# Hybrid decoder step on one core: conditioning rows turned on VectorE, page units ahead of the position products, another order at the sample attention's entry

## The chip, the cores and the metric

One core of a Trainium2 chip runs one layer of a hybrid decoder step in one launch. The metric is the device time of the whole launch in microseconds (us); lower is better.

## The reference, cut to what matters

The layer runs for a prompt of 512 tokens and for 8 samples of 8 tokens each (64 tokens), which share the weights. The conditioning vectors `c` (one of the prompt, eight of the samples) give shifts, scales and gates; the samples attend to past keys in pages.

```python
def adaln(c, w_ada, b_ada):
    mod = jax.nn.silu(c) @ w_ada + b_ada
    return jnp.split(mod[:, None, :], 6, axis=-1)

def compress(rows, pe, w1, w2):                    # over 2048 + 8 cached rows of each sample, and over the prompt
    chunks = rows[:, :n_ch * CMP_STRIDE].reshape(...)
    proj = jnp.einsum('bnkf,rfh->rbnkh', chunks, w1.reshape(r_n, CMP_STRIDE * HEAD_DIM, CMP_HIDDEN))
    pre = sum(proj[r][:, r:r + nc] for r in range(r_n)) + pe.reshape(-1) @ w1
    out = jax.nn.silu(pre) @ w2
...
    q, kc_r, vc_r, ks, vs, kw, vw, gates, u, bg = project(modulate(xs, ln1_g, sh1, sc1), pos_s, w_in, q_norm_g, k_norm_g)
    # attention: compressed blocks, 16 selected blocks of 64 keys, a window of 512; mixed by gates
    o = nsa_attend(q, pos_s, kc, vc, kc_end, ksb, vsb, kw_all, vw_all, kw_pos, gates)
    cy, s_conv = short_conv(u, state_conv, w_conv)
    xs = xs + g1 * mix_out(o, bg * cy, attn_out_g, conv_out_g, w_o)     # each part RMS-normed first
    xs = xs + g2 * swiglu(modulate(xs, ln2_g, sh2, sc2), w_gu, w_down)
```

## The kernel before

Each engine has one program, written in order by hand; engines wait for one another by semaphores. A PSUM bank is one of eight; `plan_banks` fixes for every product (a key such as `("pre", 3)`) which bank it takes and as whose successor. `want_free`, `want_filled` and `want_emptied` are waits on a bank's predecessor, its product and its evacuation; `fills` and `frees` give the marks. So an order in `plan_banks` is also an order of waits.

**Start, 0 to 130 us.** Sixteen page units u (keys and values of 8 samples in turn, 1 MB each) go through: GpSimd gathers a unit by four indirect DMAs into one of four slots (line 892), and from unit 4 on waits until unit u-4 has been turned; VectorE turns it in squares of 32 (`turn_chunks`, line 1602) into one of two buffers; TensorE forms its products with the first compression weights (`compress_first`, line 2506); ScalarE copies one half (line 1059), VectorE adds the other (`both_chunks`, line 1608), ScalarE takes the silu with the bias `pebt` (line 1067); TensorE forms the second products (`compress_second`, line 2514). Among the units stand: `turn_rows`, which turns silu(c) (`scrow`, 9 rows of 1024) by eight turns on TensorE into `cT`, and the gain rows into `colT`; `position_rows` (line 2494), 32 products of one column with 64 weight columns each that give the bias `pebt`, between units 0 and 1; eight steps with `w_ada` (line 2467), the turns of the normed tokens (line 2432), and in VectorE's step 13 the modulation of all tokens. Then come the projections with pairs of high and low weights (lines 2438 to 2440), first of attention, then of the convolution (`cv`, n 0 to 2, m 0 to 3, two halves h).

**Middle, 250 to 292 us.** During the last third (n = 2: the gate blocks `("cv", 2, m, h)`) the work of the sample attention begins between the blocks: units 16 and 17 (the prompt's), queries placed, compressed scores, their softmax (`cmp_probs`), its turn (`cmp_turn`) and values. VectorE multiplies each block into `vT` (line 1861) and gives `y_ready`; ScalarE squares it. `turn_page(gp, b)` (line 1826) turns a page of selected keys; (0, 0) overwrites the compression weights and so waits for unit 17's products. Behind the last block TensorE makes the query copies `qR`, importance and values, turns the new keys (`kTn`), and sums the squares of the convolution output (`yss`, line 2830); ScalarE takes the roots. Then `scores(0)` (line 2708).

**Groups, 288 to 380 us.** Four groups gp of two samples: scores, window scores, exponentials on ScalarE (line 1238), turned probabilities `("PT", gp, i)`, compressed scores of the next group, importance (`imp`, line 1800), ranking, two steps with `w_ada`, next scores, values. Group 0 also holds the norm of the prompt's compressed keys (`norm_inverse(2)`, `norm_apply(11)`, lines 1697 to 1719) and their turn (`turn_blocks(2)`). SP's queue loads tokens, weights and states; it waits in order too.

## Time and profile before

| | us |
|---|---|
| three runs | 923.3, 924.52, 925.25 (median 924.52) |
| the profiled execution's own time | 924.75 |
| its span, first to last instruction | 922.9 |
| TensorE busy | 854.2 (93%) |
| VectorE, ScalarE, GpSimd busy | 622.8, 372.8, 307.5 |

In the page's slices each digit is a fortieth of the span, 23 us. In a timeline row the bracket names how long the engine stood idle just before and what ended that; "remote" or "issue" means that the profile shows no releaser. Recorded ends of products on TensorE are modelled.

### The profile page before, as it was taken

How to read it: one execution, taken by the hardware profiler on the slowest of the kernel's cores; microseconds unless marked ns; L12 is line 12 of the kernel's file. 1: busy time of each engine (PE TensorE's matmuls, PEld its weight loads, DVE VectorE, ACT ScalarE, POOL GpSimd, SP SyncE). 2: the span in 40 equal slices, each digit the busy share in tenths (PEclk: the TensorE clock that was granted, in tenths of full speed). 3: DMA queues.
4: the chain of work that ended last, by engine and by line, in shares of the span. 5: the costliest groups of instructions: out<-in, count | busy, mean ns of one | idle time of the engine just before them, and what ended most of it. 6: DMA issues, size and time to landing. Idle time of an engine off the chain costs nothing.

```text
span 922.9 us, 17110 instructions
## 1 busy us (share of the span) xinstructions
PE 854.2 (93%) x6689; PEld 733.0 (79%) x6689; DVE 622.8 (67%) x1219; ACT 372.8 (40%) x751; POOL 307.5 (33%) x303
## 2 busy tenths in 40 slices
PE   3498999999988789899999998999999999999998
PEld 2366778899976556676777798999999999888886
DVE  2156585388945775758486899888888888434444
ACT  1033252141234343767843664444444446223221
POOL 6465400000003321535500318777766773000000
PEclk9699999999988788999999999999999999999999
DMA  7988913236276798294102453333333324422201
GB/s 207 344 306 313 317 47 99 94 110 243 68 263 249 277 376 301 51 316 138 36 1 92 129 147 107 98 101 104 95 93 93 93 92 153 156 92 92 74 1 52
DMA packets 89166, 138.88 MB, mean 150 GB/s; under 512 B 9267, under 2 KB 59987, under 8 KB 84798
## 3 DMA queue, kind: packets, MB, share of 16 engines
q1 hardware_dynamic: 74866, 96.26, 32.6%
q0 software_dynamic: 9376, 40.31, 12.2%
q10 hardware_dynamic: 4844, 1.21, 0.6%
q8 instruction: 54, 0.88, 0.4%
q14 instruction: 26, 0.21, 0.1%
HBM read 130.58 MB, written 11.31 MB: 154 GB/s over the span
## 4 chain that ended last, share of the span: by engine, by line
PE 78%; DVE 8%; issue 7%; ACT 3%; another core or an unknown queue 1%; POOL 1%; DVEq 0%; ACTq 0%; POOLq 0%
PE bank L2438 18%; PE bank L2440 18%; PE bank L2439 18%; PE bank L2432 4%; PE bank L2506 4%; PE bank L2794 2%; PE bank L2708 2%; PE bank L2926 2%; PE bank L2467 2%; PE bank L2448 2%; PE bank L2447 2%; PE bank L2958 2%; PE bank L2764 1%; DVE mem L1602 1%
## 5 line engine op out<-in xcount | busy, mean ns | idle before, releaser
L2438 PE MATMUL bank<-s,ring_hi 128*128 128x288 f32 x620 | 184.7, 298 | 3.7 <-DVE ring_lo L536 3.7
L2439 PE MATMUL bank<-s,ring_lo 128*128 128x288 f32 x620 | 183.6, 296 | 0.0
L2440 PE MATMUL bank<-s,ring_hi 128*128 128x288 f32 x620 | 183.0, 295 | 0.0
L2438 PEld LDWEIGHTS bank<-s,ring_hi 128*128 128x128 f32 x620 | 116.8, 188 | 4.6 <-DVE ring_lo L536 4.5
L2440 PEld LDWEIGHTS bank<-s,ring_hi 128*128 128x128 f32 x620 | 117.5, 190 | 0.0
L2439 PEld LDWEIGHTS bank<-s,ring_lo 128*128 128x128 f32 x620 | 117.0, 189 | 0.0
L536 DVE TENSOR_TENSOR ring_lo<-mem,ring_hi 128x512 fp32r<-128x512 f32 x84 | 106.3, 1301 | 2.1 <-POOL mem L988 1.8
L536 DVE TENSOR_TENSOR dn_w<-wring,dn_w 128x2048 fp32r<-128x2048 f32 (+1 forms) x11 | 23.1, 2096 | 65.9 <-ACT dn_w L533 65.9
L2438 PE MATMUL bank<-dn_w,dn_hi 128*128 128x512 f32 x160 | 62.2, 389 | 0.0
L2439 PE MATMUL bank<-dn_w,dn_lo 128*128 128x512 f32 x160 | 62.2, 389 | 0.0
L2440 PE MATMUL bank<-dn_w,dn_hi 128*128 128x512 f32 x160 | 62.2, 389 | 0.0
L901 POOL DMA_INDIRECT arena<-in_cache_k_slc,idx x8 | 7.9, 988 | 157.3 <-PE bank L2440 148.1
L2438 PE MATMUL bank<-hhi,ws 128*128 128x288 f32 x192 | 58.0, 302 | 0.0
L2439 PE MATMUL bank<-h1hi,ws 128*128 128x288 f32 x192 | 57.6, 300 | 0.0
L2440 PE MATMUL bank<-h1hi,ws 128*128 128x288 f32 x192 | 57.6, 300 | 0.0
L533 ACT CAST dn_w<-wring 128x2048 fp32r<-128x2048 f32 (+1 forms) x11 | 19.3, 1757 | 83.0 <-PE bank L2440 83.0
L536 DVE TENSOR_TENSOR ring_lo<-wring,ring_hi 128x512 fp32r<-128x512 f32 x71 | 52.4, 743 | 0.5 <-ACT ring_hi L533 0.5
L533 ACT CAST ring_hi<-mem 128x512 fp32r<-128x512 f32 x84 | 49.9, 617 | 6.5 <-POOL mem L980 2.3
L980 POOL TENSOR_TENSOR mem<-wring 128x512 f32<-128x512 f32 x20 | 26.8, 1338 | 55.6 <-PE bank L2440 31.9
L533 ACT CAST ws<-wring 128x1024 fp32r<-128x1024 f32 (+2 forms) x18 | 21.8, 1246 | 48.4 <-PE bank L2448 27.2
L892 POOL DMA_INDIRECT arena<-in_cache_k_cmp,idq x32 | 31.5, 984 | 27.9 <-DVE uvT L1602 15.4
L533 ACT CAST ring_hi<-wring 128x512 fp32r<-128x512 f32 x71 | 39.8, 616 | 0.0
(444 smaller groups left out, 2126.5 us busy)
## 6 DMA issues: line engine op xcount, KB each, us to landing
wring<-in_w_gu SPq DMA_DIRECT2D x44, 512.0 KB
wring<-in_w_ada SPq DMA_DIRECT2D x16, 1024.0 KB
wring<-in_w_in SPq DMA_DIRECT2D x10, 1024.0 KB
wring<-in_w_down SPq DMA_DIRECT2D x10, 1024.0 KB
wring<-in_w_ada SPq DMA_DIRECT2D x16, 512.0 KB
proj<-in_x_prompt SPq DMA_DIRECT2D x4, 512.0 KB
mem<-in_state_k_win POOLq DMA_DIRECT2D x8, 256.0 KB
mem<-in_state_v_win POOLq DMA_DIRECT2D x8, 256.0 KB, 7.5
```

The lines of the kernel that those rows point to most:

```text
L533: return copy(dst, src)
L536: return eng.tensor_tensor(dst, src, hi.bitcast(F32), ALU.subtract)
L892: pool.indirect_dma_start(cring[:, slot_of(i), 512 * n:512 * n + 512], None, a[name].rearrange("l n (c i s) k d -> (l n c i) (s k d)", i=4 ...
L980: ins = pool.tensor_tensor(dst, block_of(f, 0), block_of(f, 1), ALU.subtract)
L2432: return pe.transpose(dst, src, ident[0:P, 0:P])
L2438: pe.matmul(dst, sh, ml, start=first and k == 0, stop=False)
L2439: pe.matmul(dst, sl, mh, start=False, stop=False)
L2440: ins = pe.matmul(dst, sh, mh, start=False, stop=last and k == len(pairs) - 1)
L2447: pe.matmul(dst, s, ml, start=first and k == 0, stop=False)
L2448: ins = pe.matmul(dst, s, mh, start=False, stop=last and k == len(pairs) - 1)
L2467: ins = pe.matmul(ps(key)[32 * j:32 * j + 32, :], cT[:, 32 * kk:32 * kk + 32], w[:, j, :], start=kk == 0, stop=kk == 7)
L2506: ins = pe.matmul(dst, w1v[:, u % 2, j].rearrange("p r h -> p (r h)"), x[:, j // 2, j % 2], start=j == 0, stop=j == 7)
```

## The change

Conditioning rows: `crow` is laid out as 128 x 256 (four groups of 32 partitions, nine used in each), loaded by eight DMAs of SP in place of two, cleared first by VectorE; one VectorE transpose of it makes `cT`. ScalarE issues the value weights ahead of the gain rows. Start: VectorE turns two units ahead and does so first in each step; units 0 to 2 stand ahead of the position products, which are 16 of 128 weight columns by 2 columns, and whose two parts VectorE adds; second products run two units behind. Middle: the turn of the first key page is moved from m = 1 to the end of m = 2, that of the second in between the last block's two halves; the turn of the new keys stands before the importance; query copies stand before the last square on ScalarE. The squares are summed fully by VectorE ahead of TensorE, and TensorE's sum, the roots and the norm's root move into group 0, behind the turned probabilities; `norm_apply(11)` and `turn_blocks(2)` move to group 1. Two exponentials of one column are added on ScalarE.

```diff
@@ -146,18 +146,19 @@
-        if u == 0:
-            start += [("cT",), ("rows",)]
...
-        if u == 0:
+        if u == 1:
+            start.append(("rows",))
+        if u == 2:
...
-        if u:
-            start.append(("cmp", u - 1))
+        if u >= 2:
+            start.append(("cmp", u - 2))
+    start.append(("cmp", 14))
@@ -173,8 +174,7 @@
-                    ring += [("qR", i) for i in range(4)] + [("imp", 0)]
-    ring += [("kTn",), ("yss", 0), ("yss", 1)]
+                    ring += [("qR", i) for i in range(4)] + [("kTn",), ("imp", 0)]
@@ -189,8 +189,8 @@
-            ring += [("PT", gp, i) for i in range(4)] + [("cPT", gp + 1)] + [("PT", gp, i) for i in range(4, 6)] + [("imp", gp + 1)]
-            ring += [("kct", 2)] * (gp == 0) + keyed(gp + 1)
+            ring += [("PT", gp, i) for i in range(4)] + [("cPT", gp + 1)] + [("PT", gp, i) for i in range(4, 6)]
+            ring += [("yss", h) for h in range(2)] * (gp == 0) + [("imp", gp + 1)] + [("kct", 2)] * (gp == 1) + keyed(gp + 1)
@@ -312,7 +312,7 @@
-        crow, scrow = hbuf[0:9, 2 * D:3 * D], hbuf[0:9, D:2 * D]
+        crow, scrow = hbuf[:, 2048:2304], hbuf[:, 1024:1280]
@@ -372,7 +372,7 @@
-        pebt = sb("pebt", 2, parts=64)
+        pebt = sb("pebt", 4, parts=64)
@@ -682,8 +682,11 @@
-            sp.dma_start(crow[0:1, :], a["c_prompt"]).then_inc(c_loaded, 16)
-            sp.dma_start(crow[1:9, :], a["c_sample"]).then_inc(c_loaded, 16)
+            sp.wait_ge(c_cleared, 1)
+            for q in range(4):
+                for r0, n, name in ((0, 1, "c_prompt"), (1, 8, "c_sample")):
+                    sp.dma_start(crow[32 * q + r0:32 * q + r0 + n, :].rearrange("b (k r) -> b k r", r=32),
+                                 a[name].rearrange("b (k q r) -> q b k r", q=4, r=32)[q]).then_inc(c_loaded, 16)
@@ -1029,6 +1032,9 @@
+            hidden_load(1)
+            for x, w in enumerate(("w_ck2", "w_cv2")):
+                act.dma_start(w2[:, 64 * x:64 * x + 64], a[w][0]).then_inc(comp_w_loaded, 16)
@@ -1042,11 +1048,8 @@
-            hidden_load(1)
-            for x, w in enumerate(("w_ck2", "w_cv2")):
-                act.dma_start(w2[:, 64 * x:64 * x + 64], a[w][0]).then_inc(comp_w_loaded, 16)
...
-            act.wait_ge(c_loaded, 32)
+            act.wait_ge(c_loaded, 128)
@@ -1064,6 +1067,8 @@
+                if u < 2:
+                    want_emptied(act, ("peb", u))
@@ -1183,6 +1188,10 @@
+                if m == 3:
+                    for i in range(4):
+                        want_filled(act, ("qR", i))
+                        frees(act.copy(qR[i // 2][i % 2], ps(("qR", i))[:, 0:256]), ("qR", i))
@@ -1216,15 +1225,8 @@
-            for i in range(4):
-                want_filled(act, ("qR", i))
-                frees(act.copy(qR[i // 2][i % 2], ps(("qR", i))[:, 0:256]), ("qR", i))
...
-            nrm(2)
-            for h in range(2):
-                want_filled(act, ("yss", h))
-                frees(act.activation(yrs[:, HALF * h:HALF * h + HALF], ps(("yss", h))[:, 0:HALF], ACT.Sqrt,
-                                     bias=epst[:, 0:1], scale=1.0 / 512), ("yss", h))
+            act.activation(small[:, 253:254], small[:, 252:253], ACT.Exp, scale=-1.0)
@@ -1251,6 +1253,13 @@
+                    nrm(2)
+                    for h in range(2):
+                        want_filled(act, ("yss", h))
+                        frees(act.activation(yrs[:, HALF * h:HALF * h + HALF], ps(("yss", h))[:, 0:HALF], ACT.Sqrt,
+                                             bias=epst[:, 0:1], scale=1.0 / 512), ("yss", h))
+                    act.activation(small[:, 253:254], small[:, 252:253], ACT.Exp, scale=-1.0)
+                if gp == 1:
@@ -1513,11 +1522,11 @@
+            dve.memset(crow, 0.0).then_inc(c_cleared, 1)
...
-            link(dve.memset(cT[:, :], 0.0))
@@ -1610,17 +1619,21 @@
+            turn_chunks(1)
...
-                if u < 15:
-                    turn_chunks(u + 1)
-                if u >= 2:
-                    cmp_evac(u - 2)
-                if u == 0:
-                    evac(("cT",), cT[:, :].rearrange("p (k r) -> p k r", r=32)[:, :, 0:9],
-                         ps(("cT",))[:, 0:72].rearrange("p (k r) -> p k r", r=9))
+                if u < 14:
+                    turn_chunks(u + 2)
+                if u >= 3:
+                    cmp_evac(u - 3)
+                if u == 1:
...
+                    dve.wait_ge(scrow_ready, 1)
+                    dve.transpose(cT[:, :], scrow).then_inc(c_turned, 1)
...
-                        evac(("peb", x), pebt[:, x:x + 1], ps(("peb", x))[64 * x:64 * x + 64, 0:1])
+                        want_filled(dve, ("peb", x))
+                        link(dve.tensor_copy(pebt[:, 2 + x:3 + x], ps(("peb", x))[64:128, 1:2]))
+                        frees(dve.tensor_tensor(pebt[:, x:x + 1], pebt[:, 2 + x:3 + x], ps(("peb", x))[0:64, 0:1], ALU.add),
+                              ("peb", x))
@@ -1646,6 +1659,7 @@
+            cmp_evac(13)
@@ -1856,6 +1870,8 @@
+                    if m == 3 and h:
+                        turn_page(0, 1)
@@ -1870,7 +1886,6 @@
-                    turn_page(0, 0)
@@ -1881,10 +1896,12 @@
+                    turn_page(0, 0)
...
+            evac(("kTn",), kTn, ps(("kTn",))[:, 0:128].rearrange("p (x n) -> p x n", x=2))
@@ -1972,11 +1989,12 @@
-            turn_page(0, 1)
-            evac(("kTn",), kTn, ps(("kTn",))[:, 0:128].rearrange("p (x n) -> p x n", x=2))
...
+            dve.wait_ge(y_square, 4)
+            dve.tensor_tensor(yrs, hcT[:, 2, :], hcT[:, 3, :], ALU.add).then_inc(y_summed, 1)
+            dve.wait_ge(y_summed, 3)
@@ -2009,7 +2027,7 @@
-                if gp == 0:
+                if gp == 1:
@@ -2472,29 +2490,19 @@
-                pe.wait_ge(scrow_ready, 1)
-                want_free(pe, ("cT",))
-                for k in range(8):
-                    ins = turn(ps(("cT",))[:, 9 * k:9 * k + 9], scrow[:, 128 * k:128 * k + 128])
-                fills(ins, ("cT",))
...
-                pe.wait_ge(comp_w_loaded, 160)
-                want_emptied(pe, ("cT",))
...
-                ins = [None, None]
-                for i in range(16):
-                    for x in range(2):
-                        ins[x] = pe.matmul(ps(("peb", x))[64 * x:64 * x + 64, 0:1], w1v[:, x, i % 8, i // 8, :], colT[:, 36 + i:37 + i],
-                                           start=i == 0, stop=i == 15)
-                for x in range(2):
-                    fills(ins[x], ("peb", x))
+                    for j in range(8):
+                        ins = pe.matmul(ps(("peb", x))[:, 0:2], w1v[:, x, j].rearrange("p r h -> p (r h)"),
+                                        colT[:, 36:52].rearrange("p (r j) -> p j r", r=2)[:, j], start=j == 0, stop=j == 7)
+                    fills(ins, ("peb", x))
@@ -2541,11 +2549,16 @@
+                    pe.wait_ge(comp_k_loaded, 128)
+                if u == 1:
+                    pe.wait_ge(comp_w_loaded, 160)
+                compress_first(u)
+                if u == 1:
...
-                    pe.wait_ge(comp_k_loaded, 128)
-                compress_first(u)
-                if u == 0:
+                if u == 2:
...
+                if u == 4:
+                    pe.wait_ge(c_turned, 1)
@@ -2554,8 +2567,9 @@
-                if u:
-                    compress_second(u - 1)
+                if u >= 2:
+                    compress_second(u - 2)
+            compress_second(14)
@@ -2681,12 +2695,11 @@
+                            want_free(pe, ("kTn",))
+                            for x, c in enumerate((TKS, TKW)):
+                                ins = turn(ps(("kTn",))[:, 64 * x:64 * x + 64], pj[0:TS, 4, c:c + 128])
+                            fills(ins, ("kTn",))
...
-            want_free(pe, ("kTn",))
-            for x, c in enumerate((TKS, TKW)):
-                ins = turn(ps(("kTn",))[:, 64 * x:64 * x + 64], pj[0:TS, 4, c:c + 128])
-            fills(ins, ("kTn",))
@@ -2740,6 +2753,7 @@
+                want_emptied(pe, ("kTn",))
@@ -2821,18 +2835,16 @@
-            pe.wait_ge(y_summed, 2)
-            pe.wait_ge(y_square, 4)
-            for h in range(2):
-                key = ("yss", h)
-                want_free(pe, key)
-                for m in range(2, 4):
-                    last = pe.matmul(ps(key)[:, 0:HALF], cst[:, C_ONE:C_ONE + 128], hcT[:, m, HALF * h:HALF * h + HALF],
-                                     start=m == 2, stop=m == 3)
-                fills(last, key)
+            def sum_conv():
+                pe.wait_ge(y_summed, 3)
+                for h in range(2):
+                    key = ("yss", h)
+                    want_free(pe, key)
+                    fills(pe.matmul(ps(key)[:, 0:HALF], cst[:, C_ONE:C_ONE + 128], yrs[:, HALF * h:HALF * h + HALF],
+                                    start=True, stop=True), key)
...
-            want_emptied(pe, ("kTn",))
@@ -2849,10 +2861,12 @@
+                    if gp == 0:
+                        sum_conv()
...
-                    if gp == 0:
+                    if gp == 1:
```

## Rows read from the trace of the kernel before

**Rows 1.** The page: TensorE's busy time, and its busy tenths in 40 slices.
```profile
PE 854.2 (93%) x6689; PEld 733.0 (79%) x6689; DVE 622.8 (67%) x1219; ACT 372.8 (40%) x751; POOL 307.5 (33%) x303
...
PE   3498999999988789899999998999999999999998
```

**Rows 2.** Busy times by stage: window, us, then each engine, clock, DMA share, GB/s.
```profile
24.50:38.40 13.90, 1.16 (x9) 1.17 (x7) 0.00 (x0) 0.00 (x0) 7.52 (x8) 0.57 0.95 325
...
80.00:100.00 20.00, 20.00 (x117) 14.49 (x117) 13.02 (x18) 4.52 (x11) 12.40 (x12) 0.97 0.88 311
...
268.70:273.40 4.70, 0.10 (x2) 0.11 (x1) 3.65 (x9) 1.73 (x3) 0.00 (x0) 0.88 0.53 165
273.40:282.80 9.40, 9.40 (x53) 9.24 (x53) 4.58 (x12) 0.95 (x3) 0.00 (x0) 0.70 0.01 2
```

**Rows 3.** Timeline of TensorE at the start: start us, us, line, what.
```profile
17.16 6.63 PE L2506 MATMUL bank<-uvT,mem 128*128 128x256 f32 x16
23.72 0.86 PE L2494 MATMUL bank<-colT,mem 128*64 128x1 f32 x22
...
38.40 2.10 PE L2494 MATMUL bank<-colT,mem 128*64 128x1 f32 x36 [1.94 <-issue]
40.43 5.25 PE L2506 MATMUL bank<-mem 128*128 128x256 f32 x16
```

**Rows 4.** Timelines of ScalarE, SP and GpSimd at the start.
```profile
38.50 0.37 ACT L1059 COPY arena<-bank 64x254 f32<-64x254 f32 x1 [22.61 <-remote]
...
21.86 7.16 SPq L767 DMA_DIRECT2D proj<-in_x_prompt  x4
...
43.69 0.95 POOL L892 DMA_INDIRECT arena<-in_cache_k_cmp,idq  x1 [9.54 <-DVE uvT L1602]
```

**Rows 5.** Timelines of VectorE and TensorE before the last block.
```profile
268.41 2.31 DVE L1826 STREAM_TRANSPOSE mem<-arena 128x2048 f32<-128x2048 f32 x1 [7.91 <-PE bank L2506]
...
272.57 0.21 DVE L1608 TENSOR_TENSOR arena<-arena,bank 64x62 f32<-64x62 f32 x1 [0.95 <-ACT arena L1059]
...
266.48 1.89 PE L2506 MATMUL bank<-uvT,mem 128*128 128x64 f32 x16
...
273.32 0.55 PE L2432 MATMUL bank<-cst,uvT 128*127 128x128 f32 x1 [4.61 <-DVE uvT L1789]
```

**Rows 6.** ScalarE, TensorE and VectorE at the entry, and the first scores' window.
```profile
286.76 0.87 ACT L1226 ACTIVATE mem<-bank,epst 128x288 f32<-128x288 f32 x2
...
294.33 1.28 ACT L1238 ACT_TABLE_LOAD   x1
...
284.45 2.18 PE L2830 MATMUL bank<-arena,cst 128*128 128x288 f32 x8
288.09 0.58 PE L2708 MATMUL bank<-mem 32*32 32x512 f32 x1 [1.46 <-ACT mem L1226]
...
291.12 0.69 DVE L1904 CUSTOM_DVE_ANT_1 arena<-bank,selb 128x512 f32<-128x512 f32 x1 [3.22 <-PE bank L2708]
...
288.10:292.00 3.90, 3.90 (x66) 1.30 (x68) 0.88 (x3) 0.00 (x0) 1.98 (x2) 1.00 0.98 396
```

**Rows 7.** VectorE's last page transpose but one, TensorE's unit 13 and first projection product.
```profile
112.87 2.30 DVE L1602 STREAM_TRANSPOSE uvT<-arena 128x2048 f32<-128x2048 f32 x1
...
112.98 3.72 PE L2506 MATMUL bank<-mem 128*128 128x256 f32 x16
...
126.34 0.50 PE L2438 MATMUL bank<-ws,h1hi 128*128 128x512 f32 x1
```

**Rows 8.** VectorE's norm and importances in the groups, TensorE's second scores, ScalarE.
```profile
303.83 0.15 DVE L1697 RECIPROCAL hss<-hrt 128x2 f32<-128x2 f32 x1
...
326.87 0.19 DVE L1800 TENSOR_SCALAR imps<-bank 128x30 f32<-128x30 f32 x1 [0.38 <-PE bank L2633]
...
306.84 0.58 PE L2708 MATMUL bank<-mem 32*32 32x512 f32 x1 [1.20 <-DVE imps L1800]
...
305.68 0.18 ACT L1168 COPY mem<-bank 128x31 f32<-128x31 f32 x1 [3.06 <-PE bank L2432]
```

4 lines of the change are left out of this document (2 added, 2 removed).

## The prediction

> **What bounds the kernel now.** I read the page first [rows 1]: TensorE is busy 93% of the span, and the two places where its line in the slices drops are the first slice pair and the slices from 260 to 350 us. Both are where the change works, so I read those two stretches alone, by the busy times in windows [rows 2]. In 24.5 to 38.4 us TensorE is busy for 1.16 us of 13.9. In 268.7 to 273.4 us it is busy for 0.10 of 4.7, and the stretch behind that has a mean granted clock of 0.70, so that part of it ran at the lower of the two levels. From 400 us on TensorE is hardly ever idle, so a start that is earlier by some time should end the kernel earlier by as much.
>
> At the start the timeline [rows 3] shows the first page unit's products (17.16), then position products that begin at 23.72 and are all through only at 40.43. They have no wait between them; between 24.5 and 38.4 they trickle. ScalarE shows what is behind it [rows 4]: its copy of unit 0 needs only that unit's products, which are recorded as over at 23.79, yet it runs at 38.50 after 22.61 us of idle. So it is not the position products' own work that costs the time (the 36 behind 38.40 take 2.10 us, with no gap). Completions of TensorE reach the others late while GpSimd's gathers are under way: GpSimd had stood for 9.54 us when it went on at 43.69 [rows 4], so its burst of issues ended at 34.1, some 4 us before things moved again.
>
> In the middle the timeline [rows 5] shows VectorE's transpose of the first key page at 268.41: it had stood in front since 260.5, waiting for the products of unit 17, and with it stood the evacuation of the third gate block, which unit 17's hidden rows and the softmax product wait for. TensorE's turn at 273.32 waited 4.61 us for that product. At the entry [rows 6] TensorE is held until 288.09 by ScalarE's second square root, which frees the bank that the scores take (0.87 us for both roots, and a table load ahead of them). Behind it the exponentials of group 0 wait for another table load of 1.28 us at 294.33.
>
> **The change, part by part.**
>
> *Conditioning rows.* Eight turns on TensorE (about 1 us) and a copy go, a VectorE transpose of 256 columns comes. Transposes of 2048 columns take 2.30 us [rows 7], so it costs about 0.3 us, and between nothing and 0.7 in any case; it lies in VectorE's idle start. The two loads become eight, in runs of 128 bytes, on SP's queue ahead of the token loads. These wait for a gathered page and are issued from 21.86 us [rows 4], so even at 0.7 us an issue all eight are gone by 7 us. ScalarE issues the same loads in another order and is free for the silu no later. Nil.
>
> *Position products.* 32 products with 64 loaded columns become 16 with 128: the same number of loaded columns, so about the same 2 us without a stall. Half the instructions would matter if each is held for a fixed time, but they now stand behind unit 2, after the stall. Nil, bounds -1 and +1 us.
>
> *Units ahead.* Unit 0 starts when its transpose is done, some 1.5 us earlier, but is still published only when the stall ends. I keep 38.4 for that, since the gathers up to unit 5 are issued without waiting on TensorE. By then unit 1 has run too: the 5.25 us of unit 1 [rows 3] are saved. Against it: unit 2 needs VectorE's transpose, which now starts at 38.4 (2.3 us, unit 2 at 40.8, where unit 1 stood before). Then come position products (2 us), the position bias (two instructions in each of two halves on VectorE, 0.9 us), silu and the second product of unit 0 (1.5 us), and only then unit 3, at about 49.5 where it stood at 50.42. Net gain here 0.9 us. The two-unit lag of the second products spares the wait of about 1 us that one finds at later stalls: together some 2 us.
>
> *The end of that stage.* The transpose of unit u+2 now stands ahead of everything that VectorE does in step u. In step 13 this is the last transpose, and it waits for unit 13's products (over at 116.70, where the transpose before it ran at 112.87 and the modulation followed without a wait), ahead of the modulation of all tokens [rows 7]. VectorE was without a gap from 112.5 to 127 and fed the first projection at 126.34 in time; now it idles 1.6 us. I count +1.7 us. So the whole start gives about -0.3 us, which is a difference of terms that are each larger: I take 0, bounds -7.5 (two units of 3.72 us and no loss behind) and +5.
>
> *First key page moved behind the gates.* Now the evacuation of the third block runs at once. From the copy of unit 17 at 272.24 to the turn at 273.32 is 1.08 us; this chain (ScalarE's copy runs from 272.24) can start at 268.4, when the unit's products are done [rows 5]. The turn then comes at 269.5: -3.8 us. TensorE idles 1 us in place of 4.6, and I assume the clock stays at the upper level. The stretch 273.4 to 282.8 at a mean of 0.70 [rows 2] is then 9.4 x 0.70 = 6.6 us: -2.8 us. The last block is filled at about 276.3, 6.4 us earlier. What is late next is VectorE: from 269.5 it has an evacuation (0.3), the norm's sum (0.6), groups (0.6), gates (1.5), the page (2.3), sums of squares (1.55) and an evacuation (0.5), end at 277.1. That takes back 0.8 us.
>
> *The entry.* Before, scores began 5.4 us behind the last block's end. Now behind 277.1: the second page (2.3; it was behind the evacuation), evacuation and its mark (0.6), the key turn on TensorE (0.33) and its copy with the unit's (0.5), importance and value products (0.7): 4.4 us, scores at 281.5 in place of 288.09. Gone are the squares' four products (2.18 us, they are two of 1.1 later) and the wait on ScalarE. The extra sum on VectorE (0.78) lies in its wait of 3.22 us for the scores [rows 6]. Entry and block together: -6.6 us. GpSimd's value and window loads hang on the last block's end and come earlier with it; VectorE's wait for the first window was nil and stays so.
>
> *What is pushed into the groups.* In group 0 TensorE gets the two sum products (1.1 us) behind the turned probabilities, ScalarE a table load, a root, two roots of 0.87 together and a load back (3.7 us, most of it in the 3.06 us before 305.68 in which it stood idle [rows 8]), and VectorE loses the norm of 1.6 us that stood in front of the importance [rows 8]. The table for the exponentials is now loaded early, by an exponential of one column in ScalarE's idle time; the 1.28 us go from the path, but TensorE's window scores in front of the turned probabilities let it come only 0.5 us earlier. Scores of group 1 waited 1.20 us for the importance; they then wait for TensorE alone, some 305.65 for 306.84: -1.2 us. In group 1 the norm comes in behind the groups' product, in front of the window's transpose and the importance, where VectorE had 0.38 us free [rows 8]; the last score bank is now the one that importance frees: +1.3 us. Sum +0.1 us.
>
> The sum: 0 - 6.6 + 0.1 = -6.5 us. The profiled execution took 924.75 us, 0.2 above the median of 924.52; 924.75 - 6.5 = **918.2 us**.
>
> **The rivals.**
>
> *The start pays too.* If unit 0 is published before the stall sets in (its products now end at 22.3), VectorE turns unit 2 at once, and two units are done when the stall ends. Their 7.4 us come on top: 910.8. For it: the stall is seen only from 23.8 on. Against: the mark of unit 0 was among those held back, and it now stands at nearly the same time.
>
> *The clock takes it back.* The new entry leaves TensorE with little to do from 276.8 to 281.5. If it falls to the lower level there, the scores (3.9 us at the old place [rows 6], at the upper level) take some 2.3 us more; if it falls already for the 1 us idle before the last block, 2.8 us are lost again. With both the gain is 1.4 us: 923.3, no change that can be measured. For it: the level fell within a stretch of 4.7 us idle and lasted into the products. The Trainium skill's page "TensorE: Matmul & The Clock Gate", in its part on the clock gate, says that the array drops to half rate when it has been little used and comes back only after sustained use; by that rule the moved work is best where TensorE keeps busy, and the change removes filler from the entry.
>
> *Slower: the gathers don't pause.* Before, the gathers paused from 34.2 to 43.69, and the completions came through within that pause. If unit 2 is turned during the stall, GpSimd follows at once with unit 6 (four issues, 5 us), and the stall lasts 5 us longer; each later burst, now closer to its predecessor, can do that again. With two such prolongations the start loses 10 us against the 6.5 won: 928.2. It decides from 6.5 us of prolongation on. Against it: TensorE could run ahead during a stall, and in 80 to 100 us, with gathers throughout, it was busy all the time [rows 2].
>
> *The stage behind swallows it.* Pages and windows load the DMA engines at 0.98 around 290 us [rows 6]. If the values of the first groups wait for pages and these are no earlier, some 5 us go: 923.2.
>
> **How the numbers follow.** Forecast 0.52 (914.5 to 921.5, all but 0.01 faster); the start pays 0.20; the clock 0.10; swallowed 0.08; slower 0.10. A measurement tells about 0.2% (1.85 us) from no change. Faster: 0.51 + 0.20 and half of the swallowed case, 0.74; same: 0.15; slower: 0.11. The range goes from the paying start (910.8) to just above the unchanged time, 925.5; it leaves out most of the slower case and a start that pays still more.
>
> **What would show it.** First key page's transpose at about 272.8 with the turn of the softmax at 269.5, no idle stretch above 1.5 us before the last block, granted clock 1.00 there, scores 6 to 7 us earlier against the first projection's start. In group 1 the second scores wait for the importance. At the start the first projection within 2 us of 126.3, ScalarE's first copy still at about 38. If that copy comes at 23 us or at 43, the term for the start is wrong; if the first scores take 4.5 us or more, it is the clock.

## The result, and the profile after

| | before | after |
|---|---|---|
| runs of one comparison, us | 923.3 to 925.25, median 924.16 (4) | 933.18, 934.5, 938.34, 938.59, median 936.42 |
| profiled execution, own time, us | 924.75 | 933.18 |
| its span, us | 922.9 | 931.3 |

The changed kernel is slower: ratio 1.0135, 95% interval 1.0112 to 1.0158, that is 12.3 us, where the prediction said 6.5 us faster. The traced execution of after is the fastest of its four: its span is 8.4 us longer than that of before's trace, so the account below explains 8.4 us; the 3.9 us from there to the difference of the medians stand in executions that aren't traced. The page of after is nearly that of before [rows 1]: TensorE is busy 5.2 us more, and its slices say no more than that the first stage is a little emptier.

```profile
PE 859.4 (92%) x6645; PEld 735.0 (79%) x6645; DVE 624.8 (67%) x1222; ACT 373.4 (40%) x754; POOL 307.3 (33%) x303
...
PE   3298989999997788999999998999999999999998
```

So I compare the same step in both timelines. These are the rows of before that the earlier groups don't hold: TensorE's units 3 and 12, and ScalarE's first exponential in groups 0 and 1.

```profile
50.42 3.72 PE L2506 MATMUL bank<-mem 128*128 128x256 f32 x16
...
108.31 3.72 PE L2506 MATMUL bank<-uvT,mem 128*128 128x256 f32 x16
...
295.63 1.15 ACT L1238 ACTIVATE arena<-arena,small 128x1024 f32<-128x1024 f32 x1
...
312.05 1.15 ACT L1238 ACTIVATE arena<-arena,small 128x1024 f32<-128x1024 f32 x1 [5.83 <-DVE small L1989]
```

| step | before | after | difference |
|---|---|---|---|
| unit 3, products | 50.42 | 53.94 | +3.5 |
| unit 12, products | 108.31 | 115.68 | +7.4 |
| first projection [rows 7] | 126.34 | 140.08 | +13.7 |
| unit 17, products [rows 5] | 266.48 | 281.49 | +15.0 |
| exponentials of group 0 | 295.63 | 304.21 | +8.6 |
| of group 1 | 312.05 | 319.17 | +7.1 |
| of group 2 | 332.23 | 340.37 | +8.1 |
| end of the span | 922.9 | 931.3 | +8.4 |

The table splits the change in two. The start loses 13.7 us (15.0 at unit 17; the first projections ran at a lower clock). From unit 17 on the kernel wins 6.6. First the start of after: ScalarE (line 1062 is the copy of before's line 1059, 1072 the silu), VectorE (1611 is the turn of units, 1534 a copy out of a bank), GpSimd's gathers (895), TensorE (2503 position products, 2514 units).

```profile
23.93 0.37 ACT L1062 COPY arena<-bank 64x254 f32<-64x254 f32 x1 [6.91 <-remote]
50.03 0.51 ACT L1072 ACTIVATE arena<-arena,pebt 64x254 f32<-64x254 f32 x1 [25.74 <-issue]
...
23.87 2.31 DVE L1611 STREAM_TRANSPOSE uvT<-arena 128x2048 f32<-128x2048 f32 x1 [3.10 <-remote]
...
43.53 2.31 DVE L1611 STREAM_TRANSPOSE mem<-arena 128x2048 f32<-128x2048 f32 x1 [17.05 <-remote]
45.76 0.17 DVE L1534 COPY colT<-bank 128x52 f32<-128x52 f32 x1
...
34.46 0.95 POOL L895 DMA_INDIRECT arena<-in_cache_k_cmp,idq  x1 [0.30 <-issue]
...
38.22 0.95 POOL L895 DMA_INDIRECT arena<-in_cache_k_cmp,idq  x1 [0.30 <-issue]
46.11 0.94 POOL L895 DMA_INDIRECT arena<-in_cache_v_cmp,idq  x1 [6.94 <-DVE mem L1611]
...
45.99 6.99 PE L2503 MATMUL bank<-colT,mem 128*128 128x2 f32 x32 [16.03 <-DVE colT L1534]
...
53.94 5.99 PE L2514 MATMUL bank<-mem 128*128 128x256 f32 x16
```

Unit 0 was published at 23.93, not at 38.4 as in [rows 4]. VectorE turned unit 2 at 23.87, and with that GpSimd went on with unit 6 at 34.46 without a pause; its last issue ended at 39.2. The next completions came through at 43.5: the trace has TensorE's semaphore marks of unit 1, of the turned gain rows and of unit 2 at 43.50, 43.54 and 43.70, though the last of these products is recorded as over at 29.96. The last recorded landing of unit 3's gather is at 27.31, so VectorE didn't wait for that. I call such a delay of TensorE's completions the hold. Then VectorE turned unit 3 and only then copied the gain rows (45.76), for which the position products stood in wait, and these took 6.99 us.

The end of the stage in after: VectorE (1569 row sum of the conditioning bias) and TensorE (2450 turns, 2456 the first projection product).

```profile
119.44 2.31 DVE L1611 STREAM_TRANSPOSE uvT<-arena 128x2048 f32<-128x2048 f32 x1 [2.11 <-PE bank L2514]
...
121.85 0.67 DVE L1569 TENSOR_TENSOR arows<-bank,arows 128x512 f32<-128x512 f32 x1
...
129.20 2.31 DVE L1611 STREAM_TRANSPOSE mem<-arena 128x2048 f32<-128x2048 f32 x1 [3.45 <-PE bank L2514]
...
115.68 3.72 PE L2514 MATMUL bank<-uvT,mem 128*128 128x256 f32 x16
122.67 0.63 PE L2450 MATMUL bank<-cst,arows 128*128 128x128 f32 x4 [3.27 <-DVE arows L1569]
...
124.11 5.06 PE L2514 MATMUL bank<-mem 128*128 128x256 f32 x16
...
140.08 0.50 PE L2456 MATMUL bank<-ws,h1hi 128*128 128x512 f32 x1
```

The turn of unit 14 (119.44) waited for the products of unit 12. The row sum stood behind it, and TensorE's turn of the modulation, which stands ahead of unit 13, waited for the row sum: 3.27 us idle, and unit 13 then took 5.06 us in place of 3.72 [rows 7]. The turn of unit 15 waited for it till 129.20, with all of the modulation behind.

The middle of after, against [rows 5, 6, 8]: TensorE's unit 17 and the turn of the softmax, VectorE's first key page and first masked scores, ScalarE's first exponentials (line 1240), and busy times in windows (columns as in [rows 2]).

```profile
281.49 1.89 PE L2514 MATMUL bank<-uvT,mem 128*128 128x64 f32 x16
...
284.52 0.35 PE L2450 MATMUL bank<-cst,uvT 128*127 128x128 f32 x1 [0.79 <-DVE uvT L1803]
...
287.98 2.31 DVE L1840 STREAM_TRANSPOSE mem<-arena 128x2048 f32<-128x2048 f32 x1
...
301.31 0.69 DVE L1921 CUSTOM_DVE_ANT_1 arena<-bank,selb 128x512 f32<-128x512 f32 x1 [1.44 <-PE bank L2721]
...
304.21 1.15 ACT L1240 ACTIVATE arena<-arena,small 128x1024 f32<-128x1024 f32 x1
...
319.17 1.15 ACT L1240 ACTIVATE arena<-arena,small 128x1024 f32<-128x1024 f32 x1 [3.82 <-DVE small L2007]
...
288.30:291.80 3.50, 3.27 (x27) 2.94 (x25) 3.43 (x4) 0.00 (x0) 0.27 (x1) 1.00 0.00 0
291.80:298.00 6.20, 2.81 (x60) 1.56 (x76) 4.43 (x11) 2.49 (x7) 5.03 (x7) 0.69 0.75 255
298.00:302.00 4.00, 3.67 (x68) 1.08 (x36) 2.36 (x9) 1.19 (x2) 0.97 (x1) 0.63 1.02 420
```

### The profile page after: what moved, and what is told of

Same layout as the page of the kernel before. It is cut to its first block, busy times and chain, and to the rows that moved or that the text cites. A ratio compares the mean times of both kernels' runs of the same rounds, so it can differ in the third digit from the quotient of the medians.

```text
span 931.3 us, 17037 instructions
## 1 busy us (share of the span) xinstructions
PE 859.4 (92%) x6645; PEld 735.0 (79%) x6645; DVE 624.8 (67%) x1222; ACT 373.4 (40%) x754; POOL 307.3 (33%) x303
## 4 chain that ended last, share of the span: by engine, by line
PE 77%; DVE 9%; issue 5%; another core or an unknown queue 3%; ACT 2%; POOL 2%; DMA 1%; DVEq 0%; POOLq 0%; ACTq 0%
PE bank L2456 18%; PE bank L2458 17%; PE bank L2457 17%; PE bank L2514 4%; PE bank L2450 4%; PE bank L2721 2%; PE bank L2808 2%; PE bank L2940 2%; PE bank L2466 2%; PE bank L2465 2%; PE bank L2485 2%; PE bank L2972 1%; POOL arena L895 1%; PE bank L2778 1%
## 5 line engine op out<-in xcount | busy, mean ns | idle before, releaser
L2458 PE MATMUL bank<-h1hi,ws 128*128 128x288 f32 x192 | 56.6, 295 | 0.0
L2457 PE MATMUL bank<-h1hi,ws 128*128 128x288 f32 x192 | 56.5, 294 | 0.0
L2514 PE MATMUL bank<-uvT,mem 128*128 128x256 f32 (+1 forms) x160 | 35.9, 380 | 13.8 <-issue 12.9
L2514 PEld LDWEIGHTS bank<-uvT,mem 128*128 128x128 f32 x160 | 29.1, 201 | 18.0 <-issue 13.1
L1072 ACT ACTIVATE arena<-arena,pebt 64x254 f32<-64x254 f32 (+1 forms) x18 | 8.8, 490 | 85.7 <-PE bank L2522 30.6
```

Of the source, the lines that this page charges most:

```text
L2457: pe.matmul(dst, sl, mh, start=False, stop=False)
L2458: ins = pe.matmul(dst, sh, mh, start=False, stop=last and k == len(pairs) - 1)
L2514: ins = pe.matmul(dst, w1v[:, u % 2, j].rearrange("p r h -> p (r h)"), x[:, j // 2, j % 2], start=j == 0, stop=j == 7)
```

## Experiments

The groups ran on different chips, each beside its own runs of before, so kernels of different groups are compared by their ratios. Chip 1 is that of the result; the record doesn't name it, and it could be one of the others.

| kernel | chip | before, us | kernel, us | ratio | interval |
|---|---|---|---|---|---|
| middle_only | 2 | 926.22 | 921.64 | 0.9953 | 0.9926 to 0.9980 |
| start_only | 2 | 926.22 | 941.45 | 1.0163 | 1.0128 to 1.0198 |
| gather_paused | 2 | 926.22 | 931.31 | 1.0066 | 1.0038 to 1.0095 |
| tail_mended | 2 | 926.22 | 928.68 | 1.0023 | 0.9995 to 1.0050 |
| changed_again | 3 | 913.72 | 918.53 | 1.0047 | 1.0016 to 1.0079 |
| narrow_form | 3 | 913.72 | 918.53 | 1.0057 | 1.0031 to 1.0084 |
| all_mended | 3 | 913.72 | 912.38 | 0.9972 | 0.9949 to 0.9994 |
| weights_late | 3 | 913.72 | 905.64 | 0.9919 | 0.9880 to 0.9958 |
| before_again | 3 | 913.95 | 914.00 | 1.0003 | 0.9964 to 1.0042 |
| weights_late_2 | 3 | 913.95 | 907.71 | 0.9908 | 0.9874 to 0.9941 |
| rows_by_vector | 3 | 913.95 | 907.10 | 0.9920 | 0.9888 to 0.9951 |
| narrow_in_series | 3 | 913.95 | 906.78 | 0.9906 | 0.9869 to 0.9942 |
| middle_only_2 | 4 | 912.89 | 906.11 | 0.9937 | 0.9910 to 0.9965 |
| tail_mended_2 | 4 | 912.89 | 912.19 | 0.9991 | 0.9969 to 1.0013 |
| ahead_early | 4 | 912.89 | 906.98 | 0.9932 | 0.9907 to 0.9956 |

**The change in two halves.** The first kernel takes from the diff only the hunks of the groups, of the entry and of the last third of the projections; the second takes only the others.

> The kernel before, with the changes of the middle alone (last third of the projections, entry, groups); the start is that of before. Theory A (the loss is all in the start, and the middle gains as forecast): the first projection product stays at 126.3 us, the turn of the softmax comes at about 269.5 in place of 273.32, the first scores some 5 us earlier, and the time is 6 to 7 us below before, about 918. Theory B (the middle doesn't pay by itself: what it gained was only slack that the late start left it, or page and window loads swallow it): within 2 us of before, 922 to 926. Theory C (the middle is part of the loss): above 926.

> The changed kernel with the middle put back to that of before, so only conditioning rows, units ahead and position products are changed. Theory A: the first projection product at 140 us as in the changed kernel, everything behind it moved by the same 14 to 15 us, time 938 to 939.5. Theory B (the middle is worth nothing): equal to the changed kernel, about 936.4. Theory C (the middle loses): below 936, with the start giving less than 12 us.

Measured 4.3 us below before, and 15.1 above it. Of the two, the start is as theory A said; the middle gains less than its 6 to 7 us (interval 1.9 to 6.9), though its steps stand where they were forecast. The two ratios together (1.0163 x 0.9953 = 1.0115) give what the result shows, within the intervals. In the middle alone the turn of the softmax, the first key page and the first exponentials stand at these places (TensorE, VectorE, ScalarE); the last two lines are for the next question, ScalarE's copy of unit 0 in `middle_only` and VectorE's turn of unit 3 in `start_only`:

```profile
269.39 0.35 PE L2439 MATMUL bank<-cst,uvT 128*127 128x128 f32 x1 [0.79 <-DVE uvT L1792]
...
272.86 2.31 DVE L1829 STREAM_TRANSPOSE mem<-arena 128x2048 f32<-128x2048 f32 x1
...
289.23 1.15 ACT L1234 ACTIVATE arena<-arena,small 128x1024 f32<-128x1024 f32 x1
...
38.18 0.37 ACT L1058 COPY arena<-bank 64x254 f32<-64x254 f32 x1 [22.30 <-remote]
...
44.50 2.31 DVE L1608 STREAM_TRANSPOSE mem<-arena 128x2048 f32<-128x2048 f32 x1 [14.54 <-remote]
```

269.39 and 272.86 against the forecast of 269.5 and 272.8, and the exponentials 6.4 us ahead of 295.63.

**The pause of the gathers.**

```diff
                 if i >= CR:
-                    pool.wait_ge(turned, i - CR + 1)
+                    pool.wait_ge(turned, i - CR + 1 + (i == 6))
```

> The changed kernel, with GpSimd's gathers of page unit 6 held back until unit 3 has been turned (in place of unit 2), so that GpSimd pauses after unit 5 as it did before. Theory A (TensorE's completions are held while GpSimd's gathers run; the missing pause prolonged the stall from 38.4 to 43.5): VectorE's turn of unit 3 starts at about 38.4, the first projection some 3 to 5 us earlier than 140.1, time 931 to 933.5. Rival (what holds completions is the DMA traffic of the gathers already issued, or another load, not the issues of unit 6): turn of unit 3 still at 43 to 44, time 936 to 938. A third case: the stall does end at 38.4, but the second stall around 75 us swallows it, time 935 to 936.5.

VectorE's turn of unit 3, GpSimd's last issue of unit 5, and the first projection:

```profile
38.98 2.31 DVE L1611 STREAM_TRANSPOSE mem<-arena 128x2048 f32<-128x2048 f32 x1 [8.28 <-remote]
...
33.37 0.95 POOL L895 DMA_INDIRECT arena<-in_cache_v_cmp,idq  x1 [0.30 <-issue]
...
136.64 0.50 PE L2456 MATMUL bank<-ws,h1hi 128*128 128x512 f32 x1
```

The time is as theory A said. The last issue ended at 34.32, GpSimd went on at 41.56, and completions came through at 38.98 in place of 43.53. So these four issues did prolong the hold, by 4.5 us, and they cost 3.4 us at the first projection (136.64 for 140.08). Against `start_only`, whose start is the same and which ran on the same chip, it is 5.5 us (38.98 for 44.50) and 4.4 us (136.64 for 141.05). The ratio is 1.0066 where that of the changed kernel was 1.0135 on chip 1.

**The order of the last turns.**

```diff
-                if u < 14:
+                if u < 12:
                     turn_chunks(u + 2)
...
                     ada_rows(0)
+                    turn_chunks(14)
                 if u == 13:
                     mod_cols(0)
                     first_modulated()
+                    turn_chunks(15)
```

> The changed kernel, with VectorE's turn of unit 14 put behind the bias row sum of the conditioning weights (step 12) and the turn of unit 15 behind the modulation (step 13); the rest of the start is unchanged. Theory A (TensorE works in order, and its turn of the modulation waited 3.27 us for the row sum, which stood behind the turn of unit 14, which waited for unit 12's products): the 3.27 us of idle time go, unit 13 runs at the full clock (3.7 in place of 5.06 us), first projection about 135 in place of 140.1, time 931 to 932.5. Rival (the late gathers set the end of the stage and these waits only lie beside them): unchanged, 935.5 to 937. Without any effect of the first stall, the start up to unit 12 stays as it is (unit 12's products at 115.7).

```profile
118.01 0.67 DVE L1569 TENSOR_TENSOR arows<-bank,arows 128x512 f32<-128x512 f32 x1
120.00 2.31 DVE L1611 STREAM_TRANSPOSE uvT<-arena 128x2048 f32<-128x2048 f32 x1 [1.31 <-PE bank L2516]
...
116.24 3.72 PE L2516 MATMUL bank<-uvT,mem 128*128 128x256 f32 x16
...
134.98 0.50 PE L2458 MATMUL bank<-ws,h1hi 128*128 128x512 f32 x1
```

With the row sum (118.01) ahead of the turn of unit 14 (120.00) the stretch from unit 12 to the first projection is 18.74 us. It was 24.40 in after and 18.03 in before. The first projection comes 5.1 us earlier (134.98 for 140.08), as theory A said. The time fell by more: to 1.0023 where the whole change has 1.0135 on chip 1 and, by its two halves, 1.0115 on chip 2, that is 8.5 to 10.4 us. The two traced executions differ by 3.6 us (929.58 and 933.18), so no trace shows where the rest comes from.

**The changed kernel on another chip, the form of the position products, all parts mended, and the conditioning weights late.** `narrow_form` puts back before's 32 products of 64 weight columns, at the new place. `all_mended` joins that form, the pause, the order of the last turns, and the copy of the gain rows ahead of the turn of unit 3. `weights_late` is the middle alone with one line of SP:

```diff
+            sp.wait_ge(turned, 3)
             for i in range(WR):
                 load(i)
```

> The changed kernel itself once more, for a comparison on the chip that the other kernels of this group run on. Expected 1.0135 of before, as measured, and in the trace ScalarE's copy of unit 0 at 24 to 28 us, VectorE's turn of unit 3 at 43 to 44.5, the first projection at 139 to 141.

> The changed kernel with the position products in the form of before (32 products of one column, each with 64 weight columns, the keys' and the values' in turn, each kind in its own half of the array), but at their new place behind unit 2. The question is what 2.10 us for the last 36 records before and 6.99 us for 32 records after come from. Theory A (two products in different halves of the array run beside each other, and a load of 128 columns takes twice as long as one of 64, so the new form costs more by itself): the block takes 2 to 4 us in place of 6.99 and unit 3 starts 3 to 5 us earlier than 53.9; the time 2 to 5 us below the changed kernel. Rival (the block is slow because of its place, with the array cold and its instructions held): still near 7 us, and the time unchanged.

> The changed kernel with four of its parts mended: gathers of unit 6 held until unit 3 is turned, narrow position products, VectorE's copy of the gain rows ahead of the turn of unit 3, and the turns of units 14 and 15 behind the row sum and the modulation. Theory A (these are the places of the loss): turn of unit 3 at 39, position products over by 42 in place of 53, unit 3 at about 44 in place of 53.9, first projection between 122 and 128, so at or ahead of before's 126.3, and the time 914 to 921. Rival (the later stalls around 75 and 90 us set the end of the stage whatever comes before): first projection at 131 or later, time 924 or more.

> The kernel before with the changes of the middle, and in the start one thing: SP loads the four megabytes of conditioning weights that it issues at 30 to 34 us only once VectorE has turned unit 2 (40 us). The question is whether what holds TensorE's completions from 24 to 38.4 us is the gathers alone or all that loads the DMA engines. Theory A (the gathers alone): ScalarE's copy of unit 0 still at 38.4, time that of the middle alone, 918 to 922, or up to 2 us more where the conditioning weights come late. Rival (all the traffic together; 325 GB/s in that stretch): the copy comes 3 to 8 us earlier, as less is queued behind the token loads, and the time falls by as much, 912 to 918.

This chip gave a surprise: before took 913.7 us on it, and the changed kernel was only 4.8 us slower. TensorE in the changed kernel there (position products; unit 12; turn of the modulation; first projection):

```profile
30.12 3.73 PE L2503 MATMUL bank<-colT,mem 128*128 128x2 f32 x32 [0.84 <-DVE colT L1534]
...
98.74 3.72 PE L2514 MATMUL bank<-uvT,mem 128*128 128x256 f32 x16
105.73 1.08 PE L2450 MATMUL bank<-cst,arows 128*128 128x128 f32 x4 [3.27 <-DVE arows L1569]
...
124.64 0.50 PE L2456 MATMUL bank<-ws,h1hi 128*128 128x512 f32 x1
```

No completion was held, so the pause of the gathers told nothing here, nor did the late weights: SP came to its wait after unit 2 had been turned. That kernel therefore stands for the middle alone on this chip, 0.9919. The narrow form's block in its place:

```profile
31.60 2.13 PE L2502 MATMUL bank<-colT,mem 128*64 128x1 f32 x64 [2.64 <-DVE colT L1534]
```

2.13 us against 3.73, both at or near the upper clock (0.93 and 0.97 in their windows). So the block is as theory A said, but its gain is not: the time did not fall (1.0057 for 1.0047) and unit 3 came no earlier (35.66 for 34.82), since VectorE's turn of unit 3 waited for its gather and ended only at 31.45. On chip 1 the same 32 records took 6.99 us at the lower clock (0.50), on the path.

`all_mended` missed its mark: 0.9972, with the middle's gain in it, so its start still loses 5 us. VectorE's turn of unit 10 and the copy behind it, and TensorE's unit 9 and first projection:

```profile
78.53 2.31 DVE L1611 STREAM_TRANSPOSE uvT<-arena 128x2048 f32<-128x2048 f32 x1 [1.55 <-DMA arena<-in_cache_k_cmp,idq]
80.77 0.25 DVE L1534 COPY mem<-bank 127x128 f32<-127x128 f32 x1
...
81.07 5.41 PE L2517 MATMUL bank<-mem 128*128 128x256 f32 x16 [1.79 <-DVE mem L1534]
...
119.58 0.50 PE L2456 MATMUL bank<-ws,h1hi 128*128 128x512 f32 x1
```

The turn, two units ahead, waited 1.55 us for its gather, and the copy at 80.77 behind it held back unit 9, which took 5.41 us in place of 3.72 (granted clock 0.68). Before on the same chip (`before_again`, below) has no such wait: unit 8 stands at 72.14 there and at 72.09 here, unit 10 at 86.36 and at 89.89, so 3.5 us are lost between the two.

**Before on that chip, and three single changes on top of the middle.** `rows_by_vector` adds the conditioning rows alone (eight loads, one transpose). `narrow_in_series` adds this:

```diff
-                for i in range(16):
-                    for x in range(2):
+                for x in range(2):
+                    for i in range(16):
```

> The kernel before once more, for its trace on the chip that this group runs on. On the first two chips TensorE's completions were held in the start (ScalarE's copy of unit 0 at 38.5 and 38.2 us), on the third the changed kernel showed no hold (copy at 22.1). Expected: a chip with the hold gives the copy at 38, first projection at 126 and 924 to 927 us; one without it gives the copy at 22 to 24, first projection at 114 to 116 and 912 to 916 us.

> The kernel before with the changes of the middle, and SP's load of four megabytes of conditioning weights held until VectorE has turned unit 2. On the last chip the wait was over before SP came to it (unit 2 was turned at 27.6 us, the loads went out at 30.3), so it told nothing. On a chip with the hold: theory A (the gathers alone hold the completions) copy of unit 0 at 38 to 38.5 and 4 to 5 us below before; rival (all traffic together) the copy 3 to 8 us earlier and 8 to 13 us below before. On a chip without the hold: as the middle alone, 6 to 8 us below before.

> The kernel before with the changes of the middle and, in the start, the conditioning rows alone: cleared, loaded by eight DMAs, turned by one transpose on VectorE; position products, order of units and second products are those of before. Theory A (this part costs nothing): as the middle alone, ratio 0.992 to 0.996 of before, first projection within 1 us of before's on the same chip. Rival (the eight loads in runs of 128 bytes or the later silu hold the first gathers, TensorE or ScalarE): first projection 2 us or more later and the ratio above 0.997.

> The kernel before with the changes of the middle, and its 32 narrow position products in another order: all of the keys, then all of the values, in place of in turn. With the two kinds in turn 64 records took 2.0 to 2.13 us, where 32 records with twice the columns took 3.73 at the upper clock. Theory A (a product of the keys and one of the values run beside each other in the two halves of the array, and in series they can't): 64 records take 3.4 to 4.2 us where they aren't held. Rival (the width of the load alone makes the difference): 2.0 to 2.2 us, as in turn. The total time 0 to 2 us above that of the middle alone.

Before on chip 3, ScalarE's copy of unit 0, TensorE's unit 12 and first projection, and the window of [rows 2]:

```profile
22.80 0.37 ACT L1059 COPY arena<-bank 64x254 f32<-64x254 f32 x1 [6.92 <-PE bank L2506]
...
97.32 3.72 PE L2506 MATMUL bank<-uvT,mem 128*128 128x256 f32 x16
...
115.35 0.50 PE L2438 MATMUL bank<-ws,h1hi 128*128 128x512 f32 x1
...
24.50:38.40 13.90, 13.75 (x70) 11.34 (x69) 8.97 (x11) 5.32 (x12) 10.55 (x12) 1.00 0.96 312
```

The copy at 22.80 in place of 38.50, TensorE busy for 13.75 us of the 13.9 in which it had 1.16, with the DMA engines as busy (0.96, 312 GB/s; 0.95, 325 on chip 1). The conditioning rows cost nothing that can be told from noise (0.9920, beside 0.9908 for the kernel without them; first projection at 114.54 beside 114.87), on a chip without the hold. `weights_late_2` told nothing again, since the chip was the same: whether SP's loads take part in the hold stays open. The products in series:

```profile
22.91 3.69 PE L2501 MATMUL bank<-colT,mem 128*64 128x1 f32 x64
```

3.69 us for the same 64 records that take 2.03 in turn: a product into the lower half of the array and one into the upper half run beside each other. (In series, products that follow each other also add into the same bank, which this run does not separate.) The Trainium skill's page "TensorEngine Tiling (Array Packing)", section "Key Properties", says so: different tiles can load weights and multiply in parallel. By that page the new form, which takes the whole width, had to lose this; the traces agree.

**The last two questions, on chip 4.** `middle_only_2` and `tail_mended_2` repeat two kernels. `ahead_early` is the mended kernel with VectorE two units ahead only up to unit 3:

```diff
-                if u < 12:
+                if u < 2:
                     turn_chunks(u + 2)
+                elif 2 < u < 15:
+                    turn_chunks(u + 1)
...
```

The lines left out here put the second products one unit behind again from unit 3 on, and the turns of units 14 and 15 back to where before has them.

> The kernel before with the changes of the middle alone, once more, for the comparison within this group. Expected 4 to 8 us below before (ratio 0.991 to 0.996); on a chip without the hold of completions the first projection at 114 to 115.5 us, on one with it at 126.

> The changed kernel with the turns of units 14 and 15 behind the row sum and the modulation, once more. On a chip without the hold the changed kernel's first projection came at 124.64 us, 9.3 later than before's 115.35, and only 1.4 of that was there at the start of unit 12. Theory A (the order of VectorE's last turns is the main loss there): first projection at 118 to 120 and a ratio to before of 0.996 to 0.999, that is 5 to 8 us below the changed kernel (1.0047). Rival (the end of the stage is set by the late gathers, and mending one order only moves the wait): first projection at 123 or later, ratio 1.002 or more.

> The changed kernel with the narrow position products, the pause ahead of unit 6's gathers and the copy of the gain rows ahead of the turn of unit 3; from unit 3 on VectorE turns one unit ahead as before and the second products run one unit behind. So unlike the kernel with all four parts mended, whose ratio was 0.9972 where that of the middle alone is 0.991, only the first three units are ahead. Theory A (what the mended kernel still loses is that a turn two units ahead, waiting for its gather or its buffer, stands in VectorE's queue in front of the copies that TensorE waits for, and one more second product at the end): it goes, the first projection comes within 1.5 us of that of the middle alone and the ratio is 0.989 to 0.994. Rival (the loss comes from the start of the stage: position block behind unit 2, conditioning rows): ratio 0.996 or more. On a chip with the hold theory A gives the first projection 3 us or more ahead of that of the middle alone, since unit 3 starts some 5 us earlier.

Completions weren't held here either. The order of the last turns carries 5 us (0.9991 where the changed kernel had 1.0047 on chip 3; the stretch from unit 12 to the first projection is 18.74 us once more, where the changed kernel took 25.90). The first projection itself missed its forecast of 118 to 120, at 122.43, since unit 12 came only at 103.69. What is left over the middle alone is 0.0054, 5 us, of which the wide form is at most a part: `all_mended` has the narrow one and about the same rest. Going back to one unit ahead, with the second products one unit behind, takes it away: 0.9932 beside the middle's 0.9937. Which of the two does it was not tried apart. TensorE's unit 12 and first projection in `ahead_early`:

```profile
96.39 3.72 PE L2517 MATMUL bank<-uvT,mem 128*128 128x256 f32 x16
...
114.42 0.50 PE L2456 MATMUL bank<-ws,h1hi 128*128 128x512 f32 x1
```

18.03 us between them, to the hundredth what before has. The first projection comes 4.0 us ahead of that in `middle_only_2`, which missed its own forecast (118.43 for 114 to 115.5), all of it there at unit 12 already (96.39 and 100.40). But these are single executions, the fastest of its seven (901.8) and one of the slower of the other's eleven (908.46), and the medians are alike. So the units ahead at the head of the start win nothing that can be measured where nothing is held, and cost nothing.

The middle alone beats both kernels: by its ratios it is 4.3 and 5.8 us faster than before on chips 2 and 4, and `weights_late`, which stands for it on chip 3, 7.4. Nothing tried on top of it was measurably better.

## Why the prediction was wrong, point by point

**Conditioning rows: right.** Nil within the noise, by `rows_by_vector`.

**Units ahead: the first step that failed.** "I keep 38.4 for that, since the gathers up to unit 5 are issued without waiting on TensorE." The copy of unit 0 came at 23.93. I had named this as the premise of the rival in which the start pays, and argued that the mark of unit 0 had been among those held. Why it wasn't held as long this time is open. It wasn't that its products ended earlier: in `middle_only` they end at 22.30 and are published at 38.18, in after at 22.28 and are published at 23.93. What differs is what TensorE has behind them, position products there and unit 1 here. In the three other kernels with this start on chip 2 the copy of unit 0 comes at 25.41, 27.42 and 28.15, so it is held there too, but for 3 to 6 us only. What followed was not that rival's gain but the mechanism of the slower one: VectorE turned unit 2 inside the stretch, GpSimd issued unit 6 at once, and the hold lasted to 43.5. The two rivals were one chain, and I had given them separate chances. I priced the slower one at 10 us in the start; it took 3.4 at the first projection (4.4 by the two kernels of chip 2).

**Position products: the form.** "The same number of loaded columns, so about the same 2 us without a stall", bounds -1 and +1. The wide form takes 3.73 us for 2.03 at the upper clock, and 6.99 at the lower. On chip 1, both at the lower clock (0.50), a narrow record takes 0.058 us (36 in 2.10 [rows 3]) and a wide one 0.218. So my "2 us" was a reading of 36 of the 64 narrow records at the lower clock; all 64 would take some 3.7 us there, by estimate. No row of before shows a wide load with so few columns, so bounds of 1 us were not to be had from it; and that the narrow ones go to two halves of the array stood in the code. The block's own input, the copy of the gain rows, had got behind a turn of 2.3 us: I had counted that transpose for unit 2 and not for the products.

**The end of the stage: right place, wrong size.** I counted +1.7 us, for the turn of unit 15 ahead of the modulation. It was 24.40 - 18.03 = 6.4 us on chip 1 and 7.9 on chip 3. I had followed one step of VectorE's queue (13) and not the one ahead of it (12), where the row sum stands behind the turn of unit 14, nor what TensorE has in front of unit 13: the turn of the modulation. This is the largest part of the loss that every chip shows, and it could be read off the diff and VectorE's timeline of before, where the row sum stands at 110.05 and the turn of unit 14 behind it at 112.87 [rows 7].

**What had no term.** A transpose two units ahead waits for its gather, and the copies that TensorE needs stand behind it. The trace of `all_mended` shows one such place, worth 3.5 us; the whole rest of some 5 us is gone in `ahead_early`, which has the second products one unit behind as well.

So the start lost 13.7 where I took 0 with bounds of -7.5 and +5. By differences on chip 1: 6.4 at the end of the stage; 7.4 up to unit 12, of which 3.5 goes with the pause (unit 12 at 112.19 in `gather_paused`), and the rest, 3.9, lies with the wide, late block and the turns in front of copies, and was not split on a chip with the hold.

**Middle: right.** First key page, turn of the softmax: forecast -3.8, measured 284.52 - 15.01 = 269.51 for 273.32. Entry: forecast -6.6 at the scores, measured 297.33 - 15.01 = 282.32 for 288.09, that is -5.8, and -6.4 at the exponentials behind them. Group 0: -1.2, measured -1.5. Group 1: +1.3, measured +1.0. The end of the span: -6.6 for -6.5, in one trace; by the ratios it is 4.3, 5.8 and 7.4. One thing moved inside it: around the scores the clock was 0.63 to 0.69, and from their start (297.33) to VectorE's first mask were 3.98 us where it had been 3.03 [rows 6]. So half of the rival of the clock came true, for 1 us. The other half did not: before the last block the clock stayed at 1.00.

**The chances.** The figure for faster is mis-added: 0.51 + 0.20 + 0.04 is 0.75, not 0.74.

**What stays open.** Why completions of TensorE are held on chips 1 and 2 and not on chips 3 and 4, with the same program and the same traffic; and whether SP's loads take part in it. The gathers' issues can't be all of it, since GpSimd issues as densely where nothing is held. One rival was neither named nor tested: that the recording of the execution takes part. A gathered unit gives 64 landing marks (four issues of 16). For each of units 2, 3 and 4 the six traces of chips 1 and 2 hold only 4 to 13 of them, the eleven traces of chips 3 and 4 hold 63 or 64. So the hold goes with lost records in the same stretch; whether one causes the other, or both come from a third thing, no run tells.

## What to carry to other kernels

Where an engine's work is moved ahead in its queue, list everything that then stands behind it at every step, the first and the last steps too, and ask of each who waits for it; a moved step that waits for something two units away turns slack into head-of-line waiting. Rivals that share a premise belong into one chain of events, not into separate chances. A form with fewer, wider products is no saving where the narrow ones used two parts of the array at once. And a stall that a change is built on is worth finding in a trace from a second chip first: the one at 24 to 38 us stood on some chips only.

## What the hardware showed that I had not expected

- From 24 to 38 us TensorE's completions were held on chips 1 and 2 (copy of unit 0 at 38.50 and 38.18 with before's start) and not on chips 3 and 4 (22.80 and 22.58), at 312 to 325 GB/s in all four. Before takes 924.2 and 926.2 us on the first two, 913.7 to 914 and 912.9 on the others.
- Where they are held, most come through 4 to 5 us after the end of the last gather issue: 34.2 to 38.5 (before), 34.32 to 38.98 (`gather_paused`), 39.2 to 43.5 (after), 39.3 to 44.5 (`start_only`). Not all: with unit 1 behind it, unit 0 comes through at 23.93 to 28.15, while the issues go on.
- In the traces with the hold most landing marks of the gathers of that stretch are missing (4 to 13 of 64 recorded), in those without it none or one.
- 64 products' records with 64 weight columns each take 2.03 us when they alternate between the halves of the array, and 3.69 us in series; 32 with 128 columns 3.73.
